# State-space core: outputs a pair later, first products and exponents inside the last gate slab, diagonals on ScalarE, the first output slab around the last pair

## The chip, the cores and the metric

One core of one Trainium2 chip runs the whole program. The metric is device microseconds of one execution, as the median of three runs. A core has five engines that run their own instruction lists in order and meet only at semaphores: TensorE (PE, matmuls into PSUM), VectorE (DVE), ScalarE (ACT), GpSimd (POOL), and SyncE (SP), which starts most transfers.

## The reference, cut to what matters

A 256-token sequence of width 1024 goes through a first network of two layers and a second one of two layers. All is float32. The change lies in one sublayer of the second network, the bidirectional state-space mixer (32 heads of 64, 8 groups of 4 heads, state 128, chunks of 128 tokens):

```python
proj = h @ w_in
z, xbc, dt_raw = jnp.split(proj, [D_INNER, D_INNER + SSD_CONV_CH], axis=-1)
xbc = jax.nn.silu(depthwise_conv_centred(xbc, conv_w, conv_b))
xs, Bm, Cm = jnp.split(xbc, [...], axis=-1)
...
y_fwd = ssd_chunked(xs, dt[:, :, 0], A[0], Bm, Cm)
y_bwd = flip(ssd_chunked(flip(xs), flip(dt[:, :, 1]), A[1], flip(Bm), flip(Cm)))
y = y_fwd + y_bwd + xs * d_skip.reshape(g, r)[..., None]
y = y.reshape(b, s, D_INNER) * jax.nn.silu(z)
y = rms_norm_2(y.reshape(b, s, g, SSD_NORM_GROUP), norm_g.reshape(g, SSD_NORM_GROUP))
return y.reshape(b, s, D_INNER) @ w_out
```

For every head the core needs exp of differences of a running sum (the decay), times the product C B of its group, and that matrix times the head's inputs. Then come the skip term, the gate silu(z), a norm over each group of 256 channels, and the output product.

## The kernel before, in words

Weights come from memory in slabs of 1 MB (128 x 2048). To keep float32 accuracy, each slab is split: ACT rounds it into `hi` (`split_hi`, two halves), DVE forms the rest `lo` (`split_lo`, two halves), and PE does three products per tile (`three`, L376: hi·xh, hi·xl, lo·xh). A slab is 48 matmuls of 256 columns. There are two `hi`/`lo` buffers and four raw buffers.

The state-space sublayer has 25 input slabs (`ssd_in`), the core, and 8 output slabs (`ssd_out`). The last eight input slabs give the gate z; number 24 is the last gate slab. The order on each engine is written out by hand, and every wait is one on a counting semaphore.

The core handles heads h = 0..31, and pairs of heads:

- `expo(h)` (PE, L892): four matmuls write the exponents of a head into two PSUM banks. It waits until the head two before has been read (`decay_made`).
- `exps(h)` (ACT, L1649): four activations turn them into the buffer `EX[h % 4]`.
- DVE adds two parts of it (L2499), and multiplies with `cb(g)` from PSUM into `MT[h % 4]` (L2505).
- `cb(g)` (PE, L907): the product C B of a group of four heads.
- The outputs of a pair (PE, L979): eight matmuls of `MT` with the inputs.
- `gate_y(pair)` (DVE, L2463): skip term and gate, in place in `A1`; it counts `yz_ready`.
- `group_squares(g)` (ACT, L1718) of the two pairs of a group, `fold_squares` (POOL), `group_sums(g)` (PE, L940), a copy of the sums (DVE, L2470), `group_factors` (POOL: the reciprocal root), `diagonal(g)` (DVE, L2477: the identity times the factors), `spread(g)` (PE, L949: ones times that diagonal lays a factor over all partitions), `scale_group(g)` (DVE, L2483), `round_y(g)` (ACT, L1728: the high part of slab g's input) and `group_rest(g)` (DVE, L2490: the low part; it counts `h_ready`).

Output slab g needs group g (`h_ready`) and its own split weights (`lo_ready`). `ssd_rest(s)` (L986) is called ahead of slab s and puts the remaining spreads between the slabs:

```python
def ssd_rest(s):
    if s == 1:
        pe.wait_ge(q["yz_ready"], 16)
        for g in range(2, 6):
            spread(g)
        group_sums(SSD_G - 1)
    if s == 3:
        spread(6)
    if s == 4:
        spread(7)
```

On DVE the tail after the heads runs, among others, `scale_group(6)`, `group_rest(6)`, the split of slab 4, `scale_group(7)`, `group_rest(7)`, the split of slab 5 (L2547 to L2553). On ACT it runs `round_y(6)`, the rounding of slab 4, `round_y(7)`, the rounding of slab 5 (L1742 to L1746).

Of the kernel before, what the change touches and what calls it, by code (L numbers as in the profile page):

```python
# [24 lines left out]
P = 128  # L25
# [168 lines left out]
def build(nc, x, slabs, par, con, tab, small, cvec, pos, wmod, out):  # L194
    with ExitStack() as ctx:
# [127 lines left out]

        def ssd_count(s):

            return (q["conv_kept"], SSD_CONV[s] + 1) if s in SSD_CONV else (q["gate_kept"], SSD_GATE[s] + 1)
# [45 lines left out]
        def _(pe):  # L372
# [34 lines left out]
            def ssd_slab(s):  # L407
# [5 lines left out]
                for m in range(1 if SSD_KINDS[s] == "D" else 2):  # L413
                    pe.wait_ge(q["lo_ready"], 2 * SPLITS[n] + (2 if SSD_KINDS[s] == "D" else m + 1))
# [204 lines left out]
            def down_stage(stage, before=None):  # L619

                pe.wait_ge(q["h_ready"], HID[stage] + 1)
                for b in range(4, 8):
# [7 lines left out]
                for s in range(4 * loops, SLABS[stage] - 1):  # L630
# [288 lines left out]
            for s in range(2, 25):  # L919
# [8 lines left out]
                ssd_slab(s)  # L928
# [6 lines left out]

            pe.wait_ge(q["silu_ready"], 16)
            pe.wait_ge(*ssd_count(22))
            cb(0)

            def group_sums(g):  # L940

                pe.wait_ge(q["ysq_folded"], g + 1)
                for j in range(2):
                    at = g % 2 * 512 + j * P
                    last = mm(bank[3][:, T + j:T + j + 1], S[:, at:at + P], ones[:, 0:1],
# [11 lines left out]
            for pair in range(16):  # L957
                if pair < 15:
                    expo(2 * pair + 2)
                if pair == 0:  # L960
                    pe.wait_ge(*ssd_count(23))
                if pair % 2 == 0 and pair < 14:
                    cb(pair // 2 + 1)
                if pair % 2 and 3 <= pair < 15:
                    group_sums((pair - 3) // 2)
                if pair < 15:
                    expo(2 * pair + 3)
                if pair < 2:
                    pe.wait_ge(*ssd_count((24, 21)[pair]))
                if pair >= 2:  # L970
# [13 lines left out]
            spread(1)  # L984
# [12 lines left out]
            pe.wait_ge(q["decay_made"], SSD_H)  # L997
            down_stage("ssd_out", ssd_rest)
# [223 lines left out]
        def _(act):  # L1222
# [439 lines left out]
            for s in range(25):  # L1662
                n = N0["ssd_in"] + s
                if s < 24:
                    if s != 9:
                        split_hi(n + 3 if 1 <= s <= 8 else n + 2)
                else:
                    act.wait_ge(q["cols_ready"], 1)
                    exps(0)
                    exps(1)  # L1670
                act.wait_ge(q["slab_used"], n + 1)
# [43 lines left out]
                if s == 23:  # L1715
# [7 lines left out]
            for h in range(2, SSD_H):  # L1723
                exps(h)
                if h % 4 == 2 and h >= 6:
                    group_squares((h - 6) // 4)

# [4 lines left out]
            round_y(0)  # L1732
# [3 lines left out]
            round_y(2)  # L1736
            split_hi(N0["ssd_out"] + 2)
            round_y(3)
            round_y(4)
# [123 lines left out]
        def _(dve):  # L1863
# [541 lines left out]
            for s in range(25):  # L2405
                n = N0["ssd_in"] + s
                if s < 24 and s not in (9, 19):
# [55 lines left out]
            def gate_y(pair):  # L2463
# [3 lines left out]
                if pair % 2 and pair >= 3:  # L2467

                    dve.wait_ge(q["ysum_ready"], (pair - 1) // 2)
                    kept = v.tensor_copy(tiny[:, 61 + pair:63 + pair], bank[3][:, T:T + 2])  # L2470
                    if pair in (5, 13):
                        kept.then_inc(q["ysum_kept"], 1)
                step.link(stt(out=t, in0=XS[:, pair, :], scalar=col("skip", pair),
# [3 lines left out]
            def diagonal(g):  # L2477
                for j in range(2):
                    last = v.tensor_scalar(A2[:, g, j * P:(j + 1) * P], ident,
                                           tiny[:, 96 + 2 * g + j:97 + 2 * g + j], None, ALU.mult)  # L2480
                last.then_inc(q["ydiag_ready"], 1)

            def scale_group(g):  # L2483
                dve.wait_ge(q["yspread_ready"], g + 1)
                for k in (2 * g, 2 * g + 1):
                    last = stt(out=A1[:, k, :], in0=A1[:, k, :], scalar=col("snorm", k), in1=bank[g % 4][:, 0:T],
# [9 lines left out]
            for h in range(SSD_H):  # L2496
# [11 lines left out]
                if h % 2 and 3 <= h < 31:  # L2508
                    gate_y(h // 2 - 1)
                if h == 4:  # L2510
# [3 lines left out]
                if h == 28:  # L2514
                    dve.wait_ge(q["yroot_ready"], 1)
                    diagonal(0)
                    diagonal(1)
                if h == 30:
                    scale_group(0)

            group_rest(0)
            gate_y(14)
            gate_y(15)
# [361 lines left out]
```

## Time and profile before

| | |
|---|---|
| median of 3 runs | 1721.28 us (1720.5 to 1721.43) |
| the profiled execution | 1718.32 us, of which the span of the trace is 1716.5 us |
| PE busy over the span | 1697.9 us (99%) |
| DVE busy | 1386.1 us (81%) |
| ACT busy | 994.5 us (58%) |
| POOL busy | 26.3 us (2%) |
| last gate slab ends, core begins | 920.07 us after the span's start |
| first output slab begins | 977.55 us |
| output slabs end | 1026.73 us |

PE is busy nearly everywhere, so the time is PE's work plus the short stretches in which PE waits. A share of busy time over the whole span does not show those stretches; the windows of the core do. Busy time of pipelined matmuls overlaps, so the start of the next instruction, not the duration, tells what one costs.

### The profile page before, as it was taken

How to read it: one execution, taken by the hardware profiler on the slowest of the kernel's cores; microseconds unless marked ns; L12 is line 12 of the kernel's file. 1: busy time of each engine (PE TensorE's matmuls, PEld its weight loads, DVE VectorE, ACT ScalarE, POOL GpSimd, SP SyncE). 2: the span in 40 equal slices, each digit the busy share in tenths (PEclk: the TensorE clock that was granted, in tenths of full speed). 3: DMA queues.
4: the chain of work that ended last, by engine and by line, in shares of the span. 5: the costliest groups of instructions: out<-in, count | busy, mean ns of one | idle time of the engine just before them, and what ended most of it. 6: DMA issues, size and time to landing. Idle time of an engine off the chain costs nothing.

```text
span 1716.5 us, 29149 instructions
## 1 busy us (share of the span) xinstructions
PE 1697.9 (99%) x11414; PEld 1537.7 (90%) x11414; DVE 1386.1 (81%) x2191; ACT 994.5 (58%) x1580; POOL 26.3 (2%) x37
## 2 busy tenths in 40 slices
PE   9999999999999999999999899999999999999999
PEld 8799998999998988889998698888888888698888
DVE  5778888888888888899986879888988877866654
ACT  7565545767554655446677756553655457865542
POOL 0200000000000000000000100000000000000000
PEclk9999999999999999999999999999999999999999
DMA  9345567544557777795442056789677845045552
GB/s 359 137 153 191 195 221 293 197 163 164 188 187 274 273 288 276 278 359 188 178 175 99 24 199 256 272 289 340 257 280 280 308 163 212 27 148 195 195 180 91
DMA packets 62436, 367.06 MB, mean 214 GB/s; under 512 B 6944, under 2 KB 7328, under 8 KB 27776
## 3 DMA queue, kind: packets, MB, share of 16 engines
q1 hardware_dynamic: 61776, 362.70, 57.6%
q0 software_dynamic: 560, 3.01, 0.4%
q8 instruction: 64, 1.05, 0.2%
q14 instruction: 36, 0.29, 0.0%
HBM read 364.64 MB, written 1.05 MB: 213 GB/s over the span
## 4 chain that ended last, share of the span: by engine, by line
PE 92%; DVE 4%; ACT 2%; issue 1%; DMA 0%; DVEq 0%; ACTq 0%
PE psum L505 18%; PE psum L526 13%; PE psum L380 11%; PE psum L382 11%; PE psum L381 11%; PE psum L507 9%; PE psum L528 6%; PE psum L433 4%; PE psum L495 2%; PE psum L573 1%; PE psum L498 1%; DVE lo L1888 1%; ACT hi L1243 1%; DVE EX L2499 1%; PE psum L670 1%
## 5 line engine op out<-in xcount | busy, mean ns | idle before, releaser
L1888 DVE TENSOR_TENSOR lo<-raw,hi 128x1024 fp32r<-128x1024 f32 x522 | 621.1, 1228 | 161.2 <-ACT hi L1243 161.2
L1243 ACT ACTIVATE hi<-raw 128x1024 fp32r<-128x1024 f32 x522 | 523.0, 1051 | 342.4 <-PE psum L528 192.4
L505 PE MATMUL psum<-XHL,hi 128*128 128x512 f32 x1280 | 452.5, 399 | 0.0
L380 PE MATMUL psum<-XHL,hi 128*128 128x256 f32 x1320 | 375.7, 285 | 0.1
L381 PE MATMUL psum<-XHL,hi 128*128 128x256 f32 x1320 | 373.5, 283 | 0.0
L382 PE MATMUL psum<-XHL,lo 128*128 128x256 f32 x1320 | 373.4, 283 | 0.0
L507 PE MATMUL psum<-XHL,lo 128*128 128x256 f32 x1280 | 359.5, 281 | 0.0
L526 PE MATMUL psum<-HHL,hi 128*128 (+1 forms) x960 | 339.8, 399 | 0.4 <-DVE S L2078 0.4
L505 PEld LDWEIGHTS psum<-XHL,hi 128*128 128x128 f32 x1280 | 240.5, 188 | 59.9
L528 PE MATMUL psum<-HHL,lo 128*128 (+1 forms) x960 | 269.6, 281 | 0.0
L380 PEld LDWEIGHTS psum<-XHL,hi 128*128 128x128 f32 x1320 | 253.2, 192 | 2.5 <-issue 1.6
L381 PEld LDWEIGHTS psum<-XHL,hi 128*128 128x128 f32 x1320 | 253.2, 192 | 0.1
L382 PEld LDWEIGHTS psum<-XHL,lo 128*128 128x128 f32 x1320 | 253.2, 192 | 0.0
L507 PEld LDWEIGHTS psum<-XHL,lo 128*128 128x128 f32 x1280 | 241.8, 189 | 0.0
L526 PEld LDWEIGHTS psum<-HHL,hi 128*128 128x128 f32 x960 | 180.4, 188 | 46.0 <-DVE S L2078 1.1
L528 PEld LDWEIGHTS psum<-HHL,lo 128*128 128x128 f32 x960 | 181.4, 189 | 0.0
L2032 DVE CUSTOM_DVE_ANT_0 modw<-modw,cond 128x1024 f32<-128x1024 f32 x144 | 173.6, 1220 | 6.1 <-DMA modw<-wmod_dram 5.7
L1403 ACT ACTIVATE S<-psum 128x512 f32<-128x512 f32 x84 | 50.2, 597 | 203.8 <-PE psum L507 203.8
L2109 DVE TENSOR_TENSOR S<-psum,S 128x512 f32<-128x512 f32 x84 | 58.2, 692 | 66.9 <-ACT S L1403 66.7
L380 PE MATMUL psum<-HHL,hi 128*128 128x256 f32 x368 | 105.4, 286 | 0.4 <-DVE HHL L2584 0.4
L381 PE MATMUL psum<-HHL,hi 128*128 128x256 f32 x368 | 104.1, 283 | 0.0
L382 PE MATMUL psum<-HHL,lo 128*128 128x256 f32 x368 | 104.1, 283 | 0.0
(342 smaller groups left out, 2022.7 us busy)
## 6 DMA issues: line engine op xcount, KB each, us to landing
raw<-slabs_dram SPq DMA_DIRECT2D x269, 1024.0 KB, 5.3
modw<-wmod_dram SPq DMA_DIRECT2D x144, 512.0 KB, 5.5
raw<-slabs_dram SPq DMA_DIRECT2D x4, 512.0 KB, 7.6
A<-small_dram POOLq DMA_DIRECT2D x1, 1536.0 KB, 14.2
X<-x_dram SPq DMA_DIRECT2D x4, 256.0 KB, 4.0
out_dram<-X SPq DMA_DIRECT2D x3, 256.0 KB, 2.3
cond<-cvec_dram POOLq DMA_DIRECT2D x1, 512.0 KB, 8.9
A<-tab_dram POOLq DMA_DIRECT2D x1, 512.0 KB, 16.4
```

The source lines that it names most:

```text
L380: mm(dst, wh, xh, start=start, stop=False, skip_group_check=True)
L381: mm(dst, wh, xl, start=False, stop=False, skip_group_check=True)
L382: return mm(dst, wl, xh, start=False, stop=False, skip_group_check=True)
L433: last = mm(dst(m), raw[:, n % RAW, at], source[:, kt, 0:wide], start=(kt == 0 and (m == 0 or wide > T)), stop=False, skip_group_check=True)
L505: mm(dst, hi[:, k, j * P:(j + 1) * P], XHL[:, kt, :, :].rearrange("p a t -> p (a t)"), start=start, stop=False, skip_group_check=True)
L507: return mm(dst[:, T:2 * T], lo[:, k, j * P:(j + 1) * P], XHL[:, kt, 0, :], start=False, stop=False, skip_group_check=True)
L526: mm(bank[m].rearrange("p (a t) -> p a t", a=2), hi[:, k, j * P:(j + 1) * P], xhl, start=start, stop=False, skip_group_check=True)
L528: return mm(bank[m][:, 0:T], lo[:, k, j * P:(j + 1) * P], xhl[:, 0, :], start=False, stop=False, skip_group_check=True)
L1243: f(hi[:, k % SPLIT, at], raw[:, n % RAW, at], ACT.Copy).then_inc(q["hi_ready"], 1)
L1888: v.tensor_tensor(lo[:, k % SPLIT, at], raw[:, n % RAW, at], hi[:, k % SPLIT, at].bitcast(F32), ALU.subtract).then_inc(q["lo_ready"], 1)
L2032: v.tensor_tensor_reduce(out=w, in0=w, in1=cond[:, :], scale=1.0, scalar=0.0, op0=ALU.mult, op1=ALU.add, accum_out=MOD[:, n:n + 1]).then_i ...
L2109: v.tensor_tensor(two(dst), psum[:, b:b + 2, 0:T], two(S[:, 1024 + s % 2 * 512:1536 + s % 2 * 512]), ALU.add).then_inc(evacuated[s % 2], 1)
```

## The change

Nothing of the arithmetic is changed but who does it and when.

- The outputs of a pair are issued one turn of PE's loop later: turn `pair` makes the exponents of heads 2·pair+2 and 2·pair+3 and then the outputs of pair−1.
- `cb(0)` and `expo(2)` are issued ahead of and in the middle of the last gate slab. The last convolution's silu is done at slab 18 instead of 23, and the split of output slab 0 moves behind the first two heads (on ACT behind `exps(1)`, on DVE behind head 1).
- The squares of a group come one head later on ACT, the sums of a group one pair later, and POOL makes the factors two groups at a time.
- The diagonals move from DVE to ACT (`diagonals(k)`, two groups at a time, four copies with a scale column).
- `scale_group(0)` and `group_rest(0)` are moved into the heads. Half of output slab 0 is done ahead of the last pair's outputs, the other half behind them; the four zeroing matmuls go.
- The spreads are placed anew: 0 and 1 with the outputs of pairs 11 and 14, 2 and 3 ahead of slab 1, then 4 ahead of slab 2, 5 ahead of slab 3, 6 ahead of slab 4, 7 ahead of slab 5. The sums of groups 6 and 7 stand ahead of slab 2. Other PSUM places are used for spreads and sums.

```diff
@@ PE
+                    pe.wait_ge(q["silu_ready"], 16)
+                    pe.wait_ge(*ssd_count(22))
+                    cb(0)
+                    ssd_slab(s, lambda: expo(2))
...
-                    pe.wait_ge(q["yn_ready"], g - 3)
-                mm(bank[g % 4][:, 0:T], ones, A2[:, g, :], start=True, stop=True).then_inc(q["yspread_ready"], 1)
+                    pe.wait_ge(q["yn_ready"], g - 2)
+                mm(spread_bank(g), ones, A2[:, g, :], start=True, stop=True).then_inc(q["yspread_ready"], 1)
+
+            def outputs(pair):
+
+                if pair < 2:
+                    pe.wait_ge(*ssd_count((24, 21)[pair]))
+                else:
                     pe.wait_ge(q["yz_ready"], pair - 1)
+                if pair in (11, 14):
+                    spread(pair // 14)
+                if pair % 2 == 0 and 4 <= pair < 14:
+                    group_sums((pair - 4) // 2)
                 if pair == 15:
-                    spread(0)
-                    group_sums(6)
+                    group_sums(5)
                 pe.wait_ge(q["mt_ready"], 2 * pair + 2)
...
+            for pair in range(16):
+                if 0 < pair < 15:
+                    expo(2 * pair + 2)
+                if pair == 0:
+                    pe.wait_ge(*ssd_count(23))
+                if pair % 2 == 0 and pair < 14:
+                    cb(pair // 2 + 1)
+                if pair < 15:
+                    expo(2 * pair + 3)
+                if pair:
+                    outputs(pair - 1)
 
             def ssd_rest(s):
                 if s == 1:
+                    spread(2)
+                    spread(3)
+                if s == 2:
                     pe.wait_ge(q["yz_ready"], 16)
-                    for g in range(2, 6):
-                        spread(g)
-                    group_sums(SSD_G - 1)
-                if s == 3:
-                    spread(6)
-                if s == 4:
-                    spread(7)
+                    group_sums(6)
+                    group_sums(7)
+                    spread(4)
+                if s >= 3 and s < 6:
+                    spread(s + 2)
...
+            pe.wait_ge(q["h_ready"], HID["ssd_out"] + 1)
+            pe.wait_ge(q["lo_ready"], 2 * SPLITS[N0["ssd_out"]] + 2)
+            first_output(range(0, 4))
+            outputs(15)
             pe.wait_ge(q["decay_made"], SSD_H)
-            down_stage("ssd_out", ssd_rest)
+            first_output(range(4, KD)).then_inc(q["slab_used"], 1)
+            down_stage("ssd_out", ssd_rest, begun=1)
@@ ACT
+            for h in range(2, SSD_H):
+                exps(h)
+                if h % 4 == 3 and h >= 7:
+                    group_squares((h - 7) // 4)
+                if h in (19, 26):
+                    diagonals(h // 26)
+                if h == 28:
+                    round_y(0)
@@ DVE, behind the heads
             gate_y(14)
+            scale_group(1)
+            group_rest(1)
             gate_y(15)
...
             split_lo(N0["ssd_out"] + 1)
             scale_group(2)
+            group_rest(2)
+            scale_group(3)
             dve.wait_ge(q["ysum_ready"], 8)
+            v.tensor_copy(tiny[:, 76:80], bank[3][:, T + 2:T + 6]).then_inc(q["ysum_kept"], 1)
             split_lo(N0["ssd_out"] + 2)
             group_rest(3)
             scale_group(4)
             group_rest(4)
+            split_lo(N0["ssd_out"] + 3)
             scale_group(5)
-            split_lo(N0["ssd_out"] + 3)
             group_rest(5)
             scale_group(6)
             group_rest(6)
             split_lo(N0["ssd_out"] + 4)
             scale_group(7)
             group_rest(7)
```

**ACT in the heads.** ACT's list before, around the squares of group 1 (`EX2`, `EX3`, `EX0` are the buffers of heads 10, 11, 12; `S<-A1` are the squares):

```order
L1655 ACTIVATE EX2_58<-psum,cols 128x256 [waits mt_ready,expo_ready]
L1656 ACTIVATE EX2_58<-psum,cols 128x128
L1658 ACTIVATE EX2_58<-psum,cols 128x128 [waits expo_ready]
L1659 ACTIVATE EX2_58<-psum,cols 128x2x128
L1720 ACTIVATE S<-A1 128x512 [waits yz_ready]
L1655 ACTIVATE EX3_59<-psum,cols 128x256 [waits mt_ready,expo_ready]
```

and the same place now:

```order
L1688 ACTIVATE EX3_59<-psum,cols 128x256 [waits mt_ready,expo_ready]
L1689 ACTIVATE EX3_59<-psum,cols 128x128
L1691 ACTIVATE EX3_59<-psum,cols 128x128 [waits expo_ready]
L1692 ACTIVATE EX3_59<-psum,cols 128x2x128
L1753 ACTIVATE S<-A1 128x512 [waits yz_ready]
L1688 ACTIVATE EX0_56<-psum,cols 128x256 [waits mt_ready,expo_ready]
```

The squares, which wait for the gate of pair 3, stood between heads 10 and 11 and stand between heads 11 and 12 now.

**PE in the output stage.** PE's list before, from the spreads ahead of slab 1 on (`psum<-A,CN` is a spread, `psum<-CN,S` half of a group's sums, `psum<-HHL,hi` with waits the first matmul of a slab; the 47 others of each slab are left out):

```order
L955 MATMUL psum<-A,CN 128x256 [waits ydiag_ready,yz_ready]
L955 MATMUL psum<-A,CN 128x256 [waits ydiag_ready]
L955 MATMUL psum<-A,CN 128x256 [waits yn_ready,ydiag_ready] x2
L945 MATMUL psum<-CN,S 128x1 [waits ysq_folded]
L945 MATMUL psum<-CN,S 128x1
L380 MATMUL psum<-HHL,hi 128x256 [waits lo_ready,h_ready]
...
L955 MATMUL psum<-A,CN 128x256 [waits yn_ready,ydiag_ready]
L380 MATMUL psum<-HHL,hi 128x256 [waits lo_ready,h_ready]
...
L955 MATMUL psum<-A,CN 128x256 [waits yn_ready,ydiag_ready]
L380 MATMUL psum<-HHL,hi 128x256 [waits lo_ready,h_ready]
```

The first slab start in it is slab 1, the second slab 3 behind spread 6, the third slab 4 behind spread 7. The same stage now, from the sums ahead of slab 2 on:

```order
L959 MATMUL psum<-CN,S 128x1 [waits ysq_folded]
L959 MATMUL psum<-CN,S 128x1
L969 MATMUL psum<-A,CN 128x256 [waits yn_ready,ydiag_ready]
L390 MATMUL psum<-HHL,hi 128x256 [waits lo_ready,h_ready]
...
L969 MATMUL psum<-A,CN 128x256 [waits yn_ready,ydiag_ready]
L390 MATMUL psum<-HHL,hi 128x256 [waits lo_ready,h_ready]
...
L969 MATMUL psum<-A,CN 128x256 [waits yn_ready,ydiag_ready]
L390 MATMUL psum<-HHL,hi 128x256 [waits lo_ready,h_ready]
...
L969 MATMUL psum<-A,CN 128x256 [waits yn_ready,ydiag_ready]
L390 MATMUL psum<-HHL,hi 128x256 [waits lo_ready,h_ready]
```

The slab starts in it are slabs 2, 3, 4 and 5, each directly behind spreads 4, 5, 6 and 7.

**DVE in the output stage.** DVE's list now, from the scaling of group 6 to the split of slab 5 (`A1<-A1,PAR,psum` scales a group, `HHL<-A1,HHL` is its low part, `lo<-raw,hi` the split of a slab):

```order
L2530 SCALAR_TENSOR_TENSOR A1<-A1,PAR,psum 128x256 [waits yspread_ready]
L2530 SCALAR_TENSOR_TENSOR A1<-A1,PAR,psum 128x256
L2536 TENSOR_TENSOR HHL<-A1,HHL 128x512 [waits yh_ready]
L1935 TENSOR_TENSOR lo<-raw,hi 128x1024 [waits hi_ready] x2
L2530 SCALAR_TENSOR_TENSOR A1<-A1,PAR,psum 128x256 [waits yspread_ready]
L2530 SCALAR_TENSOR_TENSOR A1<-A1,PAR,psum 128x256
L2536 TENSOR_TENSOR HHL<-A1,HHL 128x512 [waits yh_ready]
L1935 TENSOR_TENSOR lo<-raw,hi 128x1024 [waits hi_ready] x2
```

These eight rows stand in the same order before (with other line numbers); here nothing moved.

## Rows read from the trace of the kernel before

**Rows 1.** Busy time by stretch (columns: stretch, us, PE, PEld, DVE, ACT, POOL, PEclk, DMA, GB/s)
```profile
0.00:6.00 6.00, 3.08 (x14) 3.08 (x15) 0.17 (x3) 2.93 (x6) 0.45 (x5) 1.00 0.64 188
...
920.07:977.55 57.48, 50.48 (x318) 36.17 (x316) 49.08 (x109) 46.60 (x133) 8.20 (x11) 1.00 0.02 8
...
1003.51:1026.73 23.22, 23.22 (x195) 23.19 (x194) 17.24 (x27) 12.03 (x17) 0.00 (x0) 1.00 0.75 272
```

**Rows 2.** Timeline of DVE, two pairs of heads (start, us, instruction, [idle before <- releaser])
```profile
938.87 0.43 DVE L2499 TENSOR_TENSOR EX<-EX 128x256 f32<-128x256 f32 x1 [0.89 <-ACT EX L1659]
...
939.93 0.47 DVE L2473 SCALAR_TENSOR_TENSOR S<-XS,PAR,psum 128x256 f32<-128x256 f32 x1
...
940.78 0.42 DVE L2499 TENSOR_TENSOR EX<-EX 128x256 f32<-128x256 f32 x1
...
944.27 0.69 DVE L2505 TENSOR_TENSOR S<-EX,psum 128x512 f32<-128x512 f32 x1
...
945.84 0.42 DVE L2499 TENSOR_TENSOR EX<-EX 128x256 f32<-128x256 f32 x1 [0.89 <-ACT EX L1659]
```

**Rows 3.** Timeline of ACT, the squares and the next two heads
```profile
936.96 0.63 ACT L1720 ACTIVATE S<-A 128x512 f32<-128x512 f32 x1 [0.81 <-DVE A L2475]
937.50 0.46 ACT L1655 ACTIVATE EX<-psum,cols 128x256 f32<-128x256 f32 x1
...
938.71 0.49 ACT L1655 ACTIVATE EX<-psum,cols 128x256 f32<-128x256 f32 x1
```

**Rows 4.** Timeline of PE, the core's start
```profile
920.07 1.03 PE L912 MATMUL psum<-A 128*128 128x256 f32 x4
920.75 0.53 PE L900 MATMUL psum<-acr,selr 128*128 128x384 f32 x1
...
921.51 1.02 PE L912 MATMUL psum<-A 128*128 128x256 f32 x4
...
923.09 1.08 PE L979 MATMUL psum<-S,XST 128*64 128x256 f32 x8
```

**Rows 5.** Timelines of ACT (head 2) and DVE (first gate), the core's start
```profile
921.42 0.47 ACT L1655 ACTIVATE EX<-psum,cols 128x256 f32<-128x256 f32 x1
...
925.33 0.47 DVE L2473 SCALAR_TENSOR_TENSOR S<-XS,PAR,psum 128x256 f32<-128x256 f32 x1
```

**Rows 6.** Timelines of DVE (head 31) and PE (last outputs, first output slab)
```profile
974.99 0.69 DVE L2505 TENSOR_TENSOR S<-EX,psum 128x512 f32<-128x512 f32 x1
...
975.73 1.08 PE L979 MATMUL psum<-S,XST 128*64 128x256 f32 x8 [0.61 <-DVE S L2505]
...
977.55 0.39 PE L380 MATMUL psum<-HHL,hi 128*128 128x256 f32 x1
```

**Rows 7.** Activations by line and shape, 128x128 with a scale column
```profile
L1437 ACT ACTIVATE S<-psum,tiny 128x128 f32<-128x128 f32 x8 | 3.0, 372 | 9.2 <-DVE tiny L2153 9.2
```

**Rows 8.** Timeline of PE, output stage: spreads ahead of slabs 1, 3, 4
```profile
983.41 1.89 PE L955 MATMUL psum<-A,CN 128*128 128x256 f32 x8
...
985.50 0.36 PE L380 MATMUL psum<-HHL,hi 128*128 128x256 f32 x1
...
997.09 0.59 PE L955 MATMUL psum<-A,CN 128*128 128x256 f32 x2
997.33 0.47 PE L380 MATMUL psum<-HHL,hi 128*128 128x256 f32 x1
...
1003.27 0.59 PE L955 MATMUL psum<-A,CN 128*128 128x256 f32 x2
```

**Rows 9.** Timelines of DVE and ACT, output stage: group 6, slabs 4 and 5
```profile
997.72 0.87 DVE L2486 SCALAR_TENSOR_TENSOR A<-A,PAR,psum 128x256 f32<-128x256 f32 x2 [1.01 <-PE psum L955]
...
999.16 1.99 ACT L1243 ACTIVATE hi<-raw 128x1024 fp32r<-128x1024 f32 x2
...
1000.24 2.36 DVE L1888 TENSOR_TENSOR lo<-raw,hi 128x1024 fp32r<-128x1024 f32 x2 [0.26 <-ACT hi L1243]
...
1006.42 2.36 DVE L1888 TENSOR_TENSOR lo<-raw,hi 128x1024 fp32r<-128x1024 f32 x2 [0.26 <-ACT hi L1243]
```

More of the change, by code:

```diff
@@ L321, in up_count, with group_bank, spread_bank @@
             return evacuated[s % 2], (EV0, OD0)[s % 2][name] + s // 2 + 1
+        def group_bank(g):
+            at = T + 2 * max(g - 5, 0)
+            return bank[2 if g < 5 else 3][:, at:at + 2]
+        def spread_bank(g):
+            b = (3, 2, 0, 1, 2, 0, 1, 2)[g]
+            return bank[b][:, T:2 * T] if g < 2 else bank[b][:, 0:T]
         def ssd_count(s):
@@ L413, in ssd_slab @@
                 for m in range(1 if SSD_KINDS[s] == "D" else 2):
+                    if m:
+                        between()
                     pe.wait_ge(q["lo_ready"], 2 * SPLITS[n] + (2 if SSD_KINDS[s] == "D" else m + 1))
@@ L617, in down_slab, with down_stage @@
                 return last.then_inc(q["slab_used"], 1)
-            def down_stage(stage, before=None):
+            def down_stage(stage, before=None, begun=0):
                 pe.wait_ge(q["h_ready"], HID[stage] + 1)
-                for b in range(4, 8):
+                for b in range(8 if begun else 4, 8):
                     mm(bank[b][:, 0:2], zero[:, :], zero[:, 0:2], start=True, stop=False,
@@ L629, in down_stage @@
                             down_slab(stage, s, i)
-                for s in range(4 * loops, SLABS[stage] - 1):
+                for s in range(4 * loops + begun, SLABS[stage] - 1):
                     if before is not None:
@@ L1663, in _ @@
                 n = N0["ssd_in"] + s
[L1664 to L1667, printed above, removed]
+                if s < 23 and s != 9:
+                    split_hi(n + 3 if 1 <= s <= 8 else n + 2)
+                if s == 24:
                     act.wait_ge(q["cols_ready"], 1)
@@ L1730, in round_y, with diagonals @@
                 f(HH[:, 2 * g:2 * g + 2, :], A1[:, 2 * g:2 * g + 2, :], ACT.Copy).then_inc(q["yh_ready"], 1)
-            round_y(0)
+            def diagonals(k):
+                act.wait_ge(q["yroot_ready"], k + 1)
+                for g in (2 * k, 2 * k + 1):
+                    for j in range(2):
+                        last = f(A2[:, g, j * P:(j + 1) * P], ident, ACT.Copy,
+                                 scale=tiny[:, 96 + 2 * g + j:97 + 2 * g + j])
+                    last.then_inc(q["ydiag_ready"], 1)
+            for h in range(2, SSD_H):
[6 more added lines that the diff above has]
+                    round_y(0)
             split_hi(N0["ssd_out"] + 1)
@@ L1736, in _ @@
             round_y(2)
+            diagonals(2)
             split_hi(N0["ssd_out"] + 2)
             round_y(3)
+            diagonals(3)
             round_y(4)
@@ L2406, in _ @@
                 n = N0["ssd_in"] + s
-                if s < 24 and s not in (9, 19):
+                if s < 23 and s not in (9, 19):
                     split_lo(n + 3 if 1 <= s <= 8 else n + 2)
@@ L2466, in gate_y @@
                 dve.wait_ge(q["y_ready"], pair + 1)
[L2467 to L2471, printed above, removed]
+                if pair % 2 == 0 and 4 <= pair < 14 or pair == 15:
+                    g = min((pair - 4) // 2, 5)
+                    dve.wait_ge(q["ysum_ready"], g + 1)
+                    kept = v.tensor_copy(tiny[:, 64 + 2 * g:66 + 2 * g], group_bank(g))
+                    if g % 2:
                         kept.then_inc(q["ysum_kept"], 1)
+                if pair == 11:
+                    scale_group(0)
                 step.link(stt(out=t, in0=XS[:, pair, :], scalar=col("skip", pair),
```

79 lines of the change are left out of this document (23 added, 56 removed).

## The prediction

> **What bounds the kernel now.** I read the busy shares by stretch first, then the timelines of DVE, ACT and PE through the core and the output slabs. In [rows 1] the reader is to see one odd stretch: between the last gate slab (920.07) and the first output slab (977.55) PE is busy 50.48 of 57.48 us, so some 7.0 us are idle; from 1003.51 to the end of the output slabs it is busy without a gap. So only those 7.0 us, and what hides behind them, can be won, and any new gap in the output slabs is lost in full.
>
> Who makes PE wait is DVE. Two pairs of heads take it 945.84 − 938.87 = 6.97 us [rows 2]. Its own work in them: a head 939.93 − 938.87 = 1.06, a gate 940.78 − 939.93 = 0.85, a copy of sums about 0.1; four heads and two gates are 6.0 us. The rest is the 0.89 us that it waits for ACT's exponents. [rows 3] show the ring: the squares wait 0.81 us for DVE's gate of the odd pair, the exponents of head 11 stand behind the squares, and DVE waits for those. ACT itself has only 4 x 1.21 + 0.54 = 5.4 us of work in the 6.97.
>
> **Part 1, the start: loses 1.8 us.** The last gate slab now has `cb(0)` ahead of it (920.75 − 920.07 = 0.68) and `expo(2)` in its middle (921.51 − 920.75 = 0.76) [rows 4]; PE's total is the same, but the slab ends 1.4 us later, at 921.5. The exponents of head 2 still stand on ACT behind the last gate's tanh and copy, which need that slab: before, they began 1.35 us after the slab's end [rows 5], so now at 922.9, and those of head 3 end two heads later at 925.4. The first outputs now stand on PE behind `expo(5)`, which waits for exactly these: 925.4 + 0.7, then 1.08 us of matmul, 927.2. DVE's first gate, before at 925.33 [rows 5], moves by 1.8 us. The earlier first two heads and the split of slab 0 behind them fill a time in which DVE would wait anyway. Bounds: 0.9 us (if only the slab's shift less the table of ACT counts) to 2.5.
>
> **Part 2, the heads: gain 3.9 us.** With the squares a head later ACT has delivered one more head when it comes to wait for the gate: DVE has two heads (2.1 us) in hand against the squares and one head of ACT (0.54 + 1.2), and the ring opens. From the first gate to head 31's product before: 974.99 − 925.33 = 49.7 us [rows 5, 6]. DVE's own work in that time now: 28 heads x 1.06 less the last product (0.6), 14 gates x 0.85, five copies of sums, the last gate's own product and `group_rest(0)` (0.7 and 0.6, forms of 128x512 like the product of [rows 2]) and `scale_group(0)` (0.8, [rows 9]), together 43.4 us. What waits remain? The eight scaled copies of the first two `diagonals` stand in ACT's list in front of exponents, and PE's outputs stand behind `expo`s that need those exponents. The trace has no such copy; the nearest is the 128x128 activation with a scale column, 372 ns [rows 7], about 0.27 from start to start, so 1.1 us for each four. I count both in full, 2.2 us, and 0.2 for the later outputs: 45.8 us. Bounds: 0 (ACT's slack of 0.6 us a round hides them) to 4 us. Gain 49.7 − 45.8 = 3.9, less part 1: head 31's product starts 2.1 us earlier, at 972.9.
>
> **Part 3, the first output slab: with parts 1 and 2, 3.8 us ahead.** Before, the chain was product of head 31, outputs (975.73), spread, zeroing, first output slab at 977.55 [rows 6], and slab 1 at 985.50 behind four spreads of about 0.4 and a pair of sums of about 0.5 (2.1 us from 983.41) [rows 8]. Now half of slab 0 (half of the 5.9 us from 997.33 to 1003.27, 2.9 [rows 8]) needs only group 0, whose low part DVE finishes 1.5 us ahead of head 31's product, at 971.4. So PE: 971.5 half a slab, 974.4 sums 0.5, outputs 1.0, half a slab 2.9, two spreads 0.9: slab 1 at 979.8, which is 5.7 us earlier than 985.50. Of that, 1.9 us of work is only moved behind slab 1 (spreads 4 and 5, two pairs of sums, less one that was in the heads); 3.8 us are real, and the gain of the heads is in them.
>
> **Part 4, the other output slabs: loses 9.3 us.** This decides. Before, spread 6 stood ahead of slab 3 and spread 7 ahead of slab 4. The splits of slabs 4 and 5 stand on DVE behind the scaling of groups 6 and 7, and on ACT behind their rounding. That chain is in [rows 8, 9]: spread 6 starts at 997.09, DVE scales at 997.72 (it had waited 1.01 us for the spread), ACT rounds the group and then slab 4 from 999.16, DVE splits slab 4 from 1000.24, and a half is done 1.2 us on: 4.35 us from the spread's start to the first usable half. Spread 7 likewise: 1003.27 to 1006.42 + 1.2. Before, slab 3 (997.33 to 1003.27, 5.9 us) hid the first and slab 4 the second. Now spread 6 stands directly ahead of slab 4 and spread 7 directly ahead of slab 5, DVE's list is the same, and nothing hides it: PE issues the spread (0.24) and waits 4.1 us, twice, 8.2 us. This price has hardly a bound below: every link is a row, and DVE and ACT have nothing else to do in it.
>
> A third wait is small: the split of slab 2 now stands behind the copy of the sums of group 7, which PE makes just ahead of slab 2. Slab 1 ends at 985.6; sums to 986.7, spread 4 to 987.0; DVE copies at 986.7 and has a half split at 988.0: 1.0 us (bounds 0 to 1.5). Slab 3's split stands ahead of group 5 and is in time.
>
> **The sum.** Slab 1 at 979.8, slab 2 at 988.0, slab 3 at 994.1, spread 6 at 1000.0, slab 4 at 1004.3, slab 5 at 1014.4. From slab 4's start to the stage's end took 1026.73 − 1003.51 = 23.2 us; less slab 4, 17.4 are left: end at 1031.9 against 1026.73, or −3.8 + 9.3 = +5.5 us. What follows is unchanged and shifts with it. The span goes from 1716.5 to 1722.0, the profiled execution from 1718.32 to 1723.8; the median of the runs stood 2.96 us above it, so **1726.8 us**, slower by 0.3%. Two edits I cost at nothing: the later split of output slab 0 holds back the load of output slab 4 by some 4 us, and that slab is rounded only at 999.16 [rows 9], some 80 us later; and the last silu moves to a gate slab of PE, behind whose 5.8 us ACT has time (if not, 0.6 us).
>
> **Rivals.** *The clock falls in the new waits* (12%). After a wait of 4.1 us PE might come back at 1.2 instead of 2.4 GHz; if a stretch as long as the wait ran at half speed, each would cost 2.05 more: +9.6, 1730.9 us. Against it: the granted clock is 1.00, the level of 2.4 GHz, in every row of [rows 1], also in the first 6 us, of which PE is busy 3.08, and with 7.0 us of small gaps. But no gap inside this kernel is as long as 4.1 us. The Trainium skill, "TensorE: Matmul & The Clock Gate", Part 1, says that idleness throttles the array to half rate and sustained work releases it; no run here shows that yet, and the profile after will.
>
> *The diagonals hide in ACT's slack* (10%): then 2.4 us more are won in part 2, +3.1, 1724.4 us. For it: ACT's 5.4 of 6.0 us; against: 0.6 us of slack a round takes two rounds for each 1.1, and PE's list hands a delay on at once.
>
> *The splits of slabs 4 and 5 come in time* (4%), the not slower side: if PE, as before, found them done, the waits of 8.2 go and −2.7 is left, 1718.6 us. It decides when each wait is under 2.75 us. For it speaks only that PE never waits in this stage before; against it, the order of DVE's and PE's lists.
>
> *The ring stays closed* (6%): DVE goes on waiting 0.9 us a round, because outputs that come a pair later make its gate late instead. Then part 2 gains nothing, +9.4, 1730.7 us. For it: the outputs have only some 0.3 us to spare in my walk.
>
> **How the numbers follow.** My forecast has 68%, with its own range of 1724.8 to 1729. The range of the time, 1723.5 to 1731, reaches to the hidden diagonals below and to clock and closed ring above. A difference under 0.2% (3.4 us) can't be told from none in this kernel, so slower begins at 1724.7: slower has 83% (65 of the forecast, clock 12, ring 6); same 14% (hidden diagonals 10, 3 of the forecast, 1 of the splits in time); faster 3% (the splits in time, with more won in the heads).
>
> **What would show it.** Right: PE idle some 4 us each ahead of slabs 4 and 5, put down to DVE's `lo`, and about 1 us ahead of slab 2; DVE's rounds of two pairs near 6.1 us, longer where the diagonals stand; the first gate later than 925.33, head 31's product near 973, slab 1 near 980. Wrong: slab 4 starting within 1 us of spread 6; rounds still at 7 us; a granted clock under 1.00 between 1000 and 1020.

## The result, and the profile after

The changed kernel takes **1732.05 us** (median of 6 runs, 1728.65 to 1734.92) against 1720.89 us before (6 runs, 1717.75 to 1722.0): ratio 1.0073, 95% interval 1.006 to 1.0087. The direction is as forecast, the size is not: 1726.8 had been named, 1723.5 to 1731 as the range. The profiled execution took 1729.66 us (span 1727.9, mean granted clock 0.997).

The output slabs first. The timeline of TensorE (PE) after, with start, duration, instruction and [idle before <- releaser]; L969 are the spreads, L390 begins a slab:

```profile
988.76 0.68 PE L969 MATMUL psum<-A,CN 128*128 128x256 f32 x2
990.38 0.35 PE L390 MATMUL psum<-HHL,hi 128*128 128x256 f32 x1 [0.94 <-DVE lo L1935]
...
1002.38 0.59 PE L969 MATMUL psum<-A,CN 128*128 128x256 f32 x2
1006.89 0.55 PE L390 MATMUL psum<-HHL,hi 128*128 128x256 f32 x1 [3.92 <-DVE lo L1935]
...
1015.00 0.59 PE L969 MATMUL psum<-A,CN 128*128 128x256 f32 x2
1019.52 0.55 PE L390 MATMUL psum<-HHL,hi 128*128 128x256 f32 x1 [3.92 <-DVE lo L1935]
```

These answer to [rows 8]: there slab 3 started 0.24 us behind spread 6. Now slab 4 starts 4.51 us behind it (1006.89 − 1002.38), slab 5 4.52 us behind spread 7, and slab 2 waits 0.94. The chain in the first of the waits, on VectorE (DVE) and ScalarE (ACT), as in [rows 9]:

```profile
1003.01 0.87 DVE L2530 SCALAR_TENSOR_TENSOR A<-A,PAR,psum 128x256 f32<-128x256 f32 x2 [3.42 <-PE psum L969]
1004.57 0.69 DVE L2536 TENSOR_TENSOR HHL<-A,HHL 128x512 fp32r<-128x512 f32 x1 [0.70 <-ACT HHL L1758]
1005.52 2.36 DVE L1935 TENSOR_TENSOR lo<-raw,hi 128x1024 fp32r<-128x1024 f32 x2 [0.25 <-ACT hi L1276]
...
1003.91 0.63 ACT L1758 ACTIVATE HHL<-A 128x512 fp32r<-128x512 f32 x1 [5.05 <-DVE A L2530]
1004.45 1.99 ACT L1276 ACTIVATE hi<-raw 128x1024 fp32r<-128x1024 f32 x2
```

DVE had stood idle 3.42 us for the spread, ACT 5.05 for the scaling. What [rows 1] did not have is in the windows of the same stretch (columns as in rows 1, the granted clock stands behind POOL):

```profile
1003.00:1004.00 1.00, 0.00 (x0) 0.00 (x0) 0.87 (x2) 0.09 (x1) 0.00 (x0) 1.00 0.00 0
1004.00:1005.00 1.00, 0.00 (x0) 0.00 (x0) 0.43 (x1) 1.00 (x2) 0.00 (x0) 1.00 0.00 0
1005.00:1006.00 1.00, 0.00 (x0) 0.00 (x0) 0.75 (x2) 1.00 (x2) 0.00 (x0) 0.63 0.00 0
1006.00:1007.00 1.00, 0.11 (x1) 0.14 (x1) 1.00 (x2) 0.43 (x1) 0.00 (x0) 0.50 0.00 0
...
1011.00:1012.00 1.00, 1.00 (x7) 1.00 (x6) 0.00 (x0) 0.00 (x0) 0.00 (x0) 0.50 1.07 442
1012.00:1013.00 1.00, 1.00 (x10) 1.00 (x10) 0.00 (x0) 0.00 (x0) 0.00 (x0) 0.95 0.03 8
...
1018.00:1019.00 1.00, 0.00 (x0) 0.00 (x0) 0.85 (x1) 1.00 (x3) 0.00 (x0) 0.96 0.00 0
1019.00:1020.00 1.00, 0.48 (x2) 0.51 (x3) 1.00 (x2) 1.00 (x3) 0.00 (x0) 0.50 0.00 0
```

Within the idle time the clock goes from 1.00 to 0.50, that is from 2.4 to 1.2 GHz, and stays there for some 5 us of work, in which products start 0.21 us apart (1007.46, 1007.67) instead of 0.12. Slab 4 takes 8.11 us (1015.00 − 1006.89) instead of 5.9. This agrees with the Trainium skill, "TensorE: Matmul & The Clock Gate", Part 1, which has idleness put the array at half rate.

The heads. Timeline of ACT: L1753 are the squares, one for each round of four heads, L1765 the diagonals (answers to [rows 3]):

```profile
945.58 0.63 ACT L1753 ACTIVATE S<-A 128x512 f32<-128x512 f32 x1 [0.73 <-DVE A L2525]
...
951.83 0.63 ACT L1753 ACTIVATE S<-A 128x512 f32<-128x512 f32 x1 [0.64 <-DVE A L2525]
952.37 1.26 ACT L1765 ACTIVATE A<-CN,tiny 128x128 f32<-128x128 f32 x4
...
959.25 0.63 ACT L1753 ACTIVATE S<-A 128x512 f32<-128x512 f32 x1 [0.64 <-DVE A L2525]
963.42 1.34 ACT L1765 ACTIVATE A<-CN,tiny 128x128 f32<-128x128 f32 x4
966.72 0.63 ACT L1753 ACTIVATE S<-A 128x512 f32<-128x512 f32 x1 [0.71 <-DVE A L2525]
```

A round (four heads, from squares to squares) takes 6.25, 7.42 and 7.47 us, against 6.97 before: shorter without diagonals, longer with them. ACT still waits 0.64 to 0.73 us in these squares, against 0.81 in [rows 3]. The ends of the heads, on DVE (first gate of an output, product of head 31; answer to [rows 5, 6]):

```profile
928.21 0.48 DVE L2523 SCALAR_TENSOR_TENSOR S<-XS,PAR,psum 128x256 f32<-128x256 f32 x1 [0.78 <-PE psum L986]
...
975.30 0.69 DVE L2549 TENSOR_TENSOR S<-EX,psum 128x512 f32<-128x512 f32 x1
```

That is 47.09 us, before 49.66.

This core began 0.96 us later than the forecast's 921.51, at 922.47. The same 0.96 us stand between the starts of the sublayer's second input slab (timelines of PE, before and then after), ahead of all that the change moves:

```profile
779.39 0.47 PE L495 MATMUL psum<-XHL,hi 128*128 128x256 f32 x1
...
780.35 0.47 PE L507 MATMUL psum<-XHL,hi 128*128 128x256 f32 x1
```

From there to the end of the last gate slab it is 140.68 us before and 142.12 now, the forecast's 1.44 more. In the experiments whose instructions are the same up to there, the last gate slab ends anywhere from 920.15 to 922.48. So I compare **the stage**: from the end of the last gate slab to the first product of the next stage, less what it takes before (106.66 us, and 1.44 less, 921.51 − 920.07 of [rows 4], where `cb(0)` and `expo(2)` are moved ahead of that end). The changed kernel: 1038.11 − 922.47 − 105.22 = **+10.42 us**; the forecast said +5.5.

### The profile page after: what moved, and what is told of

It reads as the page before. It is cut to its first block, busy times and chain, and to the rows that moved or that the text cites. A ratio compares the mean times of both kernels' runs of the same rounds, so it can differ in the third digit from the quotient of the medians.

```text
span 1727.9 us, 29142 instructions
## 1 busy us (share of the span) xinstructions
PE 1699.5 (98%) x11410; PEld 1540.2 (89%) x11410; DVE 1383.3 (80%) x2174; ACT 998.3 (58%) x1596; POOL 30.3 (2%) x39
## 4 chain that ended last, share of the span: by engine, by line
PE 90%; DVE 5%; ACT 3%; issue 1%; DMA 1%; DVEq 0%; SPq 0%; ACTq 0%
PE psum L517 17%; PE psum L538 11%; PE psum L390 11%; PE psum L391 11%; PE psum L392 11%; PE psum L519 9%; PE psum L540 6%; PE psum L445 4%; PE psum L507 2%; DVE lo L1935 1%; PE psum L585 1%; DMA modw<-wmod_dram 1%; PE psum L510 1%; ACT hi L1276 1%; PE psum L682 1%
## 5 line engine op out<-in xcount | busy, mean ns | idle before, releaser
L390 PE MATMUL psum<-XHL,hi 128*128 128x256 f32 x1320 | 375.9, 285 | 0.1
L390 PEld LDWEIGHTS psum<-XHL,hi 128*128 128x128 f32 x1320 | 253.2, 192 | 2.5 <-issue 1.6
L390 PE MATMUL psum<-HHL,hi 128*128 128x256 f32 x368 | 107.4, 292 | 9.8 <-DVE lo L1935 8.8
L391 PE MATMUL psum<-HHL,hi 128*128 128x256 f32 x368 | 105.7, 287 | 0.0
```

The lines of the kernel that those rows point to most:

```text
L390: mm(dst, wh, xh, start=start, stop=False, skip_group_check=True)
L391: mm(dst, wh, xl, start=False, stop=False, skip_group_check=True)
```

## The experiments

"Early" below is the changed kernel with its last three spreads a slab earlier; it is the base of most others. The stage is from one profile, the median from all runs of a kernel; before had 1720.6 to 1721.3 us beside them. The medians do not separate parts of 1 us from each other; the profiles can, since six kernels with the same heads repeat them at 47.08 to 47.11 us. "All mends" are early spreads, head 2 early, the first eight diagonals on GpSimd and the split of slab 2 ahead of the copy of the last sums; "best" is all mends with squares later.

| kernel | stage | median | ratio, 95% |
|---|---|---|---|
| early spreads | −1.19 | 1718.44 | 0.998 to 0.9999 |
| before, late spreads | +13.12 | 1732.65 | 1.0051 to 1.0084 |
| waits filled | +6.92 | 1727.23 | 1.0026 to 1.0056 |
| splits first | −0.59 | 1721.81 | 0.9995 to 1.0014 |
| early, squares back | +20.31 | 1742.02 | 1.0106 to 1.0135 |
| early, head 2 early | −2.22 | 1717.52 | 0.9972 to 0.9991 |
| early, GpSimd diagonals | −2.01 | 1718.75 | 0.9977 to 0.9994 |
| all mends | −3.05 | 1716.41 | 0.9964 to 0.9984 |
| all mends but GpSimd's | −3.64 | 1717.48 | 0.9969 to 0.9987 |
| all mends, squares later | **−5.69** | **1715.19** | 0.9948 to 0.9976 |
| early, sums unfolded | +0.42 | 1720.64 | 0.9992 to 1.001 |
| best, unfolded | −4.03 | 1715.48 | 0.9952 to 0.9979 |
| the same, ACT diagonals | −4.03 | 1716.86 | 0.9969 to 0.9987 |

**Is it the two waits, and whose place makes them?** Early spreads:

```diff
                     spread(4)
-                if s >= 3 and s < 6:
-                    spread(s + 2)
+                    spread(5)
+                if s in (3, 4):
+                    spread(s + 3)
```

> The changed kernel with the spread products of groups 5, 6 and 7 each one output slab earlier (ahead of slabs 2, 3 and 4), as they stood before. Order theory (the loss is the two waits of TensorE ahead of slabs 4 and 5 and the half clock in and behind them): both waits of 3.9 us and the stretches at 1.2 GHz go, 7.8 + 3.5 us of the changed kernel's +10.4, and the time comes out 1.5 us to 2.5 us below before, 1718.5 to 1719.5. Rival (ScalarE's sixteen diagonals and the later squares cost it, wherever TensorE waits): the scaling is late anyway, the waits reappear ahead of slab 3 or 6, and at least 6 us of the loss stays, 1727 or more. Clock-alone rival (the fall is not tied to these waits): the granted clock stays at 0.50 for about 5 us of the output stage, 1722 to 1724.

Measured 1718.44 us: the order theory. Waits of 0.51 and 0.43 us are left, the clock is 1.00:

```profile
1001.15 0.59 PE L969 MATMUL psum<-A,CN 128*128 128x256 f32 x2
1002.17 0.36 PE L390 MATMUL psum<-HHL,hi 128*128 128x256 f32 x1 [0.43 <-DVE lo L1936]
```

The other way round, before with that one part:

```diff
-                if s == 3:
-                    spread(6)
                 if s == 4:
+                    spread(6)
+                if s == 5:
                     spread(7)
```

> The kernel before with one part of the change alone: the spread products of groups 6 and 7 one output slab later, directly ahead of slabs 4 and 5; nothing else is touched. Order theory: the same two waits of about 4 us ahead of slabs 4 and 5, and 1.2 GHz granted for 3 to 8 us there: +8 for the waits, +2 to 5 for the clock, 1730 to 1735. Waits without the clock: 1728 to 1729. Rival (the lateness comes from the diagonals on ScalarE, which this kernel does not have): waits under 1 us each, 1721 to 1723.

Measured 1732.65 us, as great a loss as that of the whole change, from four lines. Its timeline of PE and its windows:

```profile
1001.48 0.59 PE L955 MATMUL psum<-A,CN 128*128 128x256 f32 x2
1005.99 0.55 PE L380 MATMUL psum<-HHL,hi 128*128 128x256 f32 x1 [3.92 <-DVE lo L1888]
...
1018.50 0.55 PE L380 MATMUL psum<-HHL,hi 128*128 128x256 f32 x1 [3.92 <-DVE lo L1888]
```

```profile
1004.00:1010.00 6.00, 4.01 (x19) 4.04 (x20) 2.73 (x3) 1.54 (x2) 0.00 (x0) 0.51 0.24 91
...
1016.00:1022.00 6.00, 3.50 (x16) 3.53 (x17) 5.52 (x8) 3.94 (x5) 0.00 (x0) 0.64 0.05 10
...
1444.00:1451.00 7.00, 7.00 (x28) 5.72 (x27) 3.44 (x7) 1.66 (x5) 0.00 (x0) 0.53 0.47 170
```

The same 3.92 us twice, without any diagonals on ACT. (The last row is another fall, far behind; see below.)

**Wait and clock apart.**

```diff
                     spread(s + 2)
+                if s in (4, 5):
+                    pe.wait_ge(q["yn_ready"], s + 2)
+                    busy(32, s - 4)
```

> The changed kernel with 32 products that nobody reads set into each of the two waits, behind the spread of groups 6 and 7, when the scaling of that group has gone by; the order of all else is the same. It tells the clock from the waits. If the half clock follows from TensorE's idle time in the waits: granted clock 1.00 in slabs 4 and 5, slab 4 back from 8.1 us to about 5.9 and slab 5 short by 1.2, time 3 to 4.5 us below the changed kernel, 1727 to 1728.5, waits (idle and filled together) unchanged at 3.9 to 4.3. If the clock falls for another reason: 0.50 as in the changed kernel, and 1731 to 1733.

Measured 1727.23 us, stage +6.92:

```profile
1000.07 0.59 PE L969 MATMUL psum<-A,CN 128*128 128x256 f32 x2
1000.31 4.12 PE L662 MATMUL psum<-maskr,identr 128*128 128x256 f32 x32
1004.59 0.35 PE L390 MATMUL psum<-HHL,hi 128*128 128x256 f32 x1 [0.16 <-DVE lo L1938]
```

```profile
1004.00:1010.00 6.00, 5.84 (x49) 5.67 (x48) 1.58 (x2) 0.13 (x1) 0.00 (x0) 1.00 0.47 176
```

Slab 4 comes 4.52 us behind the spread, as without filling, but the clock stays at 1.00. So of the +10.42 the clock is 10.42 − 6.92 = **3.5 us**, and against early spreads the waits are 6.92 + 1.19 = 8.1. The clock's price is not the same each time: in the kernel before with late spreads, which has the same two waits, it is some 4.6 us by the same reckoning (13.12, less 4.51 + 4.52 − 2 · 0.24 from spread to slab), since its second fall lasts to about 1024.5 and that of the changed kernel to about 1022.

**Is it the spread or the chain behind it?** The splits of slabs 4 and 5 put ahead of groups 6 and 7:

```diff
@@ DVE
             group_rest(5)
+            split_lo(N0["ssd_out"] + 4)
             scale_group(6)
             group_rest(6)
-            split_lo(N0["ssd_out"] + 4)
+            split_lo(N0["ssd_out"] + 5)
             scale_group(7)
@@ ACT: split_hi of slab 4 ahead of round_y(6), of slab 5 ahead of round_y(7)
```

> The changed kernel with its spread products where they stand, and the splits of slabs 4 and 5 (ScalarE's high parts, VectorE's low parts) put ahead of the work on groups 6 and 7 instead of behind it. If the wait is the chain spread, scaling, rest, rounding, split, and not the spread itself: slabs 4 and 5 find their splits made, both waits go, the clock stays at 1.00, and the time is within 1 us of the kernel with early spreads, 1718.5 to 1720.5. If the spread's place alone decides, or the high part is what is late: one of the two waits stays, 1724 to 1728.

Stage −0.59, its longest wait 0.94, ahead of slab 2: with the spreads unmoved, other orders of DVE's and ACT's lists take the loss away as well. The median of 1721.81 is above the range expected. Seven of its twelve runs lie at 1721.75 to 1723.39 with a mean clock of 0.996 or 0.997, the other five, the profiled one among them, at 1717.27 to 1720.46 with 0.998 to 1.0. The runs of before spread likewise (last section), but where the clock falls in those seven no profile shows.

**The ring.** Squares back where they stood, on top of early spreads:

```diff
-                if h % 4 == 3 and h >= 7:
-                    group_squares((h - 7) // 4)
+                if h % 4 == 2 and h >= 6:
+                    group_squares((h - 6) // 4)
```

> The kernel with early spreads (1718.4 median, its profiled run 1716.9) with the group squares put back one head earlier in ScalarE's order (behind heads 6, 10, ..., as before the change, so that ScalarE asks for an output that now comes a pair later). Ring theory (the gain in the heads comes from ScalarE no longer waiting in its squares for outputs of the pair just made): rounds without diagonals grow from 6.3 to 7 or more, ScalarE's waits in the squares grow to 1.5 us each, the heads are 2.5 to 5 us longer, profiled run 1719.5 to 1722. Rival (outputs a pair later open the ring by themselves, the squares' place is free): within 1 us of the kernel with early spreads.

Measured 1742.02 us, far beyond what I expected. ACT waits 20.1 us in the squares (5.3 in the changed kernel), PE 16.8 for the exponents (6.3 there), in pieces up to 4.1 us, and then the clock falls in the heads too:

```profile
934.81 0.69 PE L912 MATMUL psum<-acr,selr 128*128 128x384 f32 x1 [2.63 <-ACT EX L1693]
...
944.26 0.44 PE L912 MATMUL psum<-acr,selr 128*128 128x384 f32 x1 [2.17 <-ACT EX L1693]
```

```profile
940.00:945.00 5.00, 2.83 (x19) 1.85 (x18) 3.80 (x9) 2.67 (x9) 0.72 (x1) 0.97 0.00 0
945.00:950.00 5.00, 5.00 (x21) 3.67 (x20) 2.38 (x7) 2.94 (x10) 0.00 (x0) 0.50 0.00 0
```

The stage is 21.5 us longer than with early spreads; how much of that is the clock is not told apart. So outputs a pair later need squares that are later too.

**The start.** `exps(2)` ahead of the last gate's tanh:

> The kernel with early spreads, with the exponentials of head 2 put ahead of the last gate's tanh on ScalarE, since its products are made inside that gate slab. The predicted loss at the start (1.8 us) was that these products move ahead while ScalarE still meets them behind the last gate. If that is so: VectorE's wait for head 2 falls from 2.76 to about 1.5, the first gate of an output comes 1.0 to 1.5 us earlier (5.7 to about 4.5 us behind the last gate slab's end), profiled run 1715 to 1716. Rival (the start is held by the gate's activations, which are now later by 1.6): no gain or a loss of up to 0.5.

Stage 1.03 us shorter than early spreads; DVE's wait for head 2 is 1.88 us, not 2.76. Part 1's reason holds.

**The heads' missing 1.3 us.** The first eight diagonals on GpSimd; then all mends at once; then the same without GpSimd's part:

> The kernel with early spreads, with the eight diagonals that fall among the heads (groups 0 to 3) made by GpSimd, idle there, instead of ScalarE. The heads came out 1.3 us longer than forecast, with the two rounds of four heads that hold the diagonals at 7.4 and 7.5 us against 6.3 for those without. If ScalarE's 2.6 us for diagonals is what is late: those two rounds fall to 6.4 to 6.9, TensorE's waits for exponentials fall from 6.3 us to under 5, the heads end 1 to 2 us earlier, profiled run 1715 to 1716. Rival (rounds 5 and 6 are long by the spread and the scaling that VectorE and TensorE get there, whoever makes the diagonals): no gain, 1717; a loss if GpSimd beside VectorE slows VectorE's instructions, 1717.5 to 1719.

> Early spreads, head 2's exponentials early, GpSimd's diagonals, and the low parts of slab 2 ahead of VectorE's copy of the sums of groups 6 and 7 (TensorE waits 0.5 us there). If the parts add: 1.2 + 1.3 + 0.5 below the kernel with early spreads, profiled run 1713.5 to 1714.5. If they hide each other (one engine sets the heads, whichever it is): within 1.5 us of it.

> The kernel with all mends (early spreads, head 2 early, low parts of slab 2 early, GpSimd's diagonals; 1716.4 median) with the diagonals given back to ScalarE. If GpSimd's part is worth the 0.8 us that its heads were shorter by: profiled run at a clock of 1.00 0.5 to 1 us longer, 1714 to 1715, median 1717 to 1718. If GpSimd's part is worth nothing at the end: equal within 0.3 us at equal clock.

With GpSimd's diagonals the heads take 46.25 us instead of 47.09, the stage 0.82 less. The first round with diagonals falls from 7.40 to 6.56 us, as the first account has it; the second stays at 7.49, as the rival has it. The earlier split of slab 2 brings 1.42 (−2.22 to −3.64): with it both of PE's last waits are gone, 0.51 us ahead of slab 2 and 0.43 ahead of slab 4. With all mends the profile has a clock of 0.73 from 965 to 970 and so a stage of only −3.05; the parts do add in the kernel with filled sums below, −4.50.

Squares one head later still, on top of all mends:

```diff
-                if h % 4 == 3 and h >= 7:
-                    group_squares((h - 7) // 4)
+                if h % 4 == 0 and h >= 8:
+                    group_squares((h - 8) // 4)
...
+            group_squares(6)
```

> The kernel with all mends, with the group squares one head later still (behind heads 8, 12, ...), so that ScalarE's 8.1 us of waits in the squares become shorter. Ring theory, the other side of the kernel with the squares put back: the ring is open already (VectorE is busy 5.8 of 6.0 us in the rounds without diagonals), so the rounds stay at 6.3 and the time within 1 us. If ScalarE's waits still cost: rounds fall towards 6.0, 1 to 2 us off the median.

I had thought the ring open; it was not. ACT no longer waits in the squares of the rounds:

```profile
944.45 0.65 ACT L1755 ACTIVATE S<-A 128x512 f32<-128x512 f32 x1
...
950.43 0.65 ACT L1755 ACTIVATE S<-A 128x512 f32<-128x512 f32 x1
```

The round is 5.98 us, the heads 45.06. The kernel has the shortest stage and the lowest median of all, 1715.19 us; the next lowest, 1715.48, can't be told from it.

One other suspect was left, DVE's products of SBUF with SBUF beside GpSimd's folds. Without the folds (PE sums both halves itself):

```diff
-                    last = mm(to[:, j:j + 1], S[:, at:at + P], ones[:, 0:1],
-                              start=(j == 0), stop=(j == 1), skip_group_check=True)
+                    for half in range(2):
+                        at = g % 2 * 512 + half * T + j * P
+                        last = mm(to[:, j:j + 1], S[:, at:at + P], ones[:, 0:1], ...)
```

> The kernel with early spreads, without GpSimd's folds of the squares: TensorE adds both halves itself, four products of one column for a group instead of two. The heads are 1.3 us longer than forecast (first gate to head 31's product 47.1 us against 45.8), and VectorE's products of SBUF with SBUF (EX with EX) that start beside a GpSimd fold take 0.78 to 0.84 us instead of 0.42, 1.8 us in all in the changed kernel, 0.04 in the kernel before. If GpSimd's folds are that term: every such product back at 0.42 to 0.6, the heads 1.2 to 1.8 us shorter (45.3 to 45.9 us), profiled run at a clock of 1.00 1715 to 1716. If the length of these products has another cause, or they only take up VectorE's slack: heads at 46.8 or more, time within 0.4 us of early spreads.

> The best kernel so far (all mends and later squares, 1715.2 median, heads 45.1 us, 1.24 us of long products) without GpSimd's folds; its first eight diagonals stay on GpSimd. If the folds cost there too: heads 44.2 to 44.7 us, profiled run at a clock of 1.00 1711.5 to 1712.5. If the long products there come from the diagonals: heads as they were.

> As the kernel before it, with the first eight diagonals on ScalarE, so that GpSimd makes nothing but the tiny factors. If GpSimd's work costs VectorE more than ScalarE's diagonals cost the ring: heads 0.3 to 0.8 us shorter than with GpSimd's diagonals; if the diagonals still cost ScalarE 0.8 us in the ring: as much longer.

The folds are not what the heads lack. Every such product is back at 0.42 us (1.8 us in all), and the heads are no shorter, 47.36 us: DVE waits more for outputs (2.5 us instead of 1.7). The stage is 1.6 longer: 0.9 and 0.45 from PE's longer sums ahead of slab 2 and of the last outputs, 0.27 from the heads. Since the edit lengthens PE's sums, it does not show what the long products cost by themselves. The third is what settles the heads: like the first it has ACT's diagonals and no folds, its squares are a head later, and its heads take 45.38 us (its other two mends left them at 47.11). So the squares' place is worth 2.0 us there (1.2 with GpSimd's work, 46.24 to 45.06), and once ACT does not wait in them, its diagonals cost no more than GpSimd's, 45.38 us each.

**The spread of the runs.** Ten products between the column sums of the latent stage, in the kernel with all mends and in the one before:

> The kernel with all mends, with ten products of 128x256 that nobody reads set between the ten column sums (one column each) of the latent stage at about 1426 to 1428, some 440 us behind the changed stage. In the profiles that have the fall (two so far) the granted clock falls to 0.50 about 1.3 us behind those 2.2 us of sums and stays for some 6.5 us, about 3 us lost. If the runs above the fastest are that place: all runs at a clock of 0.999 to 1.00 and within 2 us of each other, + 1.2 for the products themselves, median 1714.5 to 1716. If the fall comes from elsewhere: the runs spread from 1713 to 1722 as before.

> The kernel before with the same ten products between the column sums of the latent stage and nothing else. Its runs so far lie at 1717 to 1719.5 with a clock of 0.999 to 1.00 and at 1720.8 to 1724 with 0.997 to 0.998. If that place makes the difference: the upper group goes, all runs at 1718 to 1720.5 (1.2 us for the products), a median about 1.5 us below before. If not: both groups stay, 1 us higher.

Medians 1715.71 us (ratio 0.9961 to 0.998) and 1719.93 (0.9987 to 1.0008). Not settled: of before's 27 runs beside them 18 had a clock of 0.998 or less, with the products 3 of 12, but the profile of the other kernel has the fall at the same place all the same (0.50 from 1430 to 1435).

## Why the prediction went wrong in size

- **Part 1 held.** The first gate comes 5.74 us behind the last gate slab's end; 5.7 had been named (921.5 to 927.2). Taking the cause away gave 1.03 back.
- **Part 2 failed in size by 1.3 us.** The step "the ring opens": with the squares one head later ACT was to have enough in hand. It still waited 5.3 us in them, 0.64 to 0.73 in a full round against 0.81 before, and whatever delays ACT (diagonals) or PE went round the ring. Counted were 45.8 us for the heads, measured 47.09; with the squares one more head later (and no folds) 45.38, diagonals on ACT or not. A small part is the count itself: its terms, with each copy of sums at 0.1, add up to 43.6 and not 43.4.
- **Part 3** inherits that: slab 1 at 982.02, less the 0.96 of the later start 981.06, against 979.8.
- **Part 4's waits held.** From a spread's start to its slab 4.51 and 4.52 us against 4.35, and 0.94 idle ahead of slab 2 against 1.0. The reading of the order, that the spread's new place takes away the slab that had hidden the chain, was right, and two kernels show it from both sides.
- **Part 4's price did not: a wait was priced at its length.** The forecast let PE come back at full speed and gave the falling clock 12%, since the clock stood at 1.00 through all gaps of [rows 1]. But the gaps of the core were of 1.3 us at most, the longest at the kernel's start of 2.9, and the prediction itself says that none is as long as 4.1. The evidence did not reach the case, so it could not make the rival unlikely. The rival's condition came true; its price was 3.5 us here and some 4.6 in the kernel before with late spreads, against the 4.1 that it named.

The sum: profiled execution 1729.66 against 1723.8 is 5.9 = 3.5 clock + 1.3 heads + 0.96 late start + 0.1. The allowance from profile to median, 2.96, was 2.39, so the median is 5.25 above the forecast. The prediction's two ways to its total do not agree: its slab starts end at 1031.9, which is 5.2 behind 1026.73 and not 5.5, and 8.2 and 1.0 make 9.2 for part 4, not 9.3. The other five runs of the changed kernel had mean clocks of 0.993 to 0.997, the profiled one 0.997; whether the two waits cost them more was not traced.

## What to carry to other kernels

When a producer is moved to directly ahead of its consumer, write out the chain between them on every engine; what hid it before is the price. Price a wait of TensorE of several microseconds with some of the work behind it at half the clock (here 3.5 and 4.6 us for two waits of 3.92), unless the same trace shows a gap of that length that passed at full clock. If an operation is issued later in a ring of engines, move every consumer that stands in another engine's list as well, and look whether that engine still waits in it.

## What was not expected of the hardware

- A product of SBUF with SBUF on DVE that meets one of GpSimd's folds takes up to twice as long, 0.56 to 0.84 us in the changed kernel. GpSimd and DVE there:

```profile
952.54 0.73 POOL L2758 TENSOR_TENSOR S<-S 128x256 f32<-128x256 f32 x1 [2.69 <-ACT S L1753]
...
952.77 0.78 DVE L2543 TENSOR_TENSOR EX<-EX 128x256 f32<-128x256 f32 x1
```

  It ends with 953.55 just 0.28 behind the fold's end, and takes 0.42 elsewhere; without folds all took 0.42. All six long ones end 0.28 or 0.29 us behind the end of a fold, whenever they began. The Trainium skill, "SBUF — State Buffer", section "SBUF: two separate sides", says that a DVE operation with two SBUF inputs and a GpSimd operation that reads SBUF lock each other out; the trace agrees, by these ends. What it costs this kernel is not shown: without folds the heads were no shorter, but PE's sums were longer.
- The clock also falls where PE is never idle. In the kernel with head 2 early, TensorE in the latent stage, then windows:

```profile
1426.12 2.29 PE L1050 MATMUL psum<-CN,S 128*128 128x1 f32 x20
1428.28 1.15 PE L1057 MATMUL psum<-S,CN 128*128 128x256 f32 x4
1429.36 1.22 PE L1059 MATMUL psum<-S,CN 32*128 32x256 f32 x2
```

```profile
1428.00:1429.00 1.00, 1.00 (x7) 0.93 (x7) 1.00 (x2) 1.00 (x3) 0.00 (x0) 1.00 0.97 410
1429.00:1436.00 7.00, 7.00 (x29) 6.00 (x28) 3.04 (x6) 1.25 (x4) 0.00 (x0) 0.52 0.42 150
```

  Behind twenty products of one column the clock is 0.52 for 7 us; the profile of before passes the same place at 1.00. Runs of one kernel that differ by 3 to 5 us show it in their mean clock: before 1717.58 to 1719.49 us at 1.000, 1720.92 to 1723.94 at 0.997 or 0.998. Which of the products do it stays open.
